# When a recurrent mixer asks for its next activation tiles: four of seven moved to hops of the recurrence, and one weight quarter moved into the next step

## The chip, the cores and the metric

The kernel runs on one core of one Trainium2 chip. The metric is the device time of one execution in microseconds. Three executions of the kernel before took 4308.31, 4318.29 and 4321.34 us, so the time before is their median, 4318.29 us. The profile is of a fourth execution, which took 4331.43 us.

## What the kernel computes

One layer of a streaming encoder over 2048 tokens of 1024 channels: a token mixer and then a mixture of experts. The change lies in the mixer, whose core is this (cut from the reference):

```python
h = rms_norm(x, norm1_gain[l]) * (1.0 + sc1) + sh1
p = h @ w_in                                   # 1024 -> 8 slices of 1024 columns, and 256 low-rank ones
...                                            # token shift, gates, decays from these slices
def step(state, inp):
    r_t, w_t, k_t, v_t, kk_t, a_t = inp
    sa = jnp.einsum('bhvk,bhk->bhv', state, kk_t)
    state = (state * w_t[:, :, None, :]
             - sa[..., None] * (kk_t * a_t)[:, :, None, :]
             + v_t[..., None] * k_t[:, :, None, :])
    y = jnp.einsum('bhvk,bhk->bhv', state, r_t)
    return state, y
...
merged = jax.nn.sigmoid(ga) * y_conv + jax.nn.sigmoid(gb) * y_rwkv
return merged @ w_out, v_first
```

## The kernel before

Five engines run streams of their own, written out by hand: TensorE (PE in the profile), VectorE (DVE), ScalarE (ACT), GpSimd (POOL), and SyncE (SP), which issues nearly all DMAs in order. They meet only at semaphores.

The mixer runs in 32 steps, `i = ct * 4 + g`: `ct` is one of 8 tiles of 128 channels (two heads), `g` one of 4 groups of 512 tokens. I call a step with `g = 3`, after which the channel tile changes, a *turn step* (3, 7, 11, ... 27), and count steps from 0. A step has two parts on TensorE.

- **Projections.** Eight slices of `h @ w_in`, in four pairs `pr`. A pair is one 2x2 block product done with seven half-size products (`proj(i, pr, n)`, n = 0 to 6, line L1082), which read seven activation tiles `hs[:, n]` (512 KB each, fetched from the DRAM tensor `h_s`) and seven weight tiles of `w[:, pr]`. Four weight tiles are loaded (`load_pair`, four DMAs of 256 KB), three more are sums that GpSimd makes from them (`mix_weights`, counted by `w_step`). All four pairs read the same `hs` tiles, so `hs[:, n]` is free for the next step after `proj(i, 3, n)`. The low-rank products L1010 and L1014 (`zdec`, `zaaa`) open a step, and L1044 and L1034 (`bonus`, `gup`) close the projections.
- **Recurrence.** `inverse_and_recurrence` interleaves two things: the triangular inverses of this step's 8 chunks of 64 tokens (L1203 to L1222), and the chunk-by-chunk recurrence of the step before, whose 24 *hops* are `x`, `u`, `sy` for chunks 0 to 7. Hop `u` of a chunk ends with L1131 and raises `u_done`. All of it is small 64x64 products, some 1500 matrix instructions and weight loads in a recurrence against about 510 in the projections.

SP's stream for a step is `load_step`: after `zaaa` it asks for `WAc` (low-rank input of the next step); in a turn step for the next channel tile's weights, pair by pair as the projections free them; then it stores `merged_s`; then it asks for the seven `hs` tiles as pair 3 frees them; in a turn step for pair 3's weights; and after `gup` for `GDc`. The stream of VectorE is a hardware loop over two steps, so it jumps back (L2310) at the start of an even step.

Of the kernel before, what the change touches and what calls it, by code (L numbers as in the profile page):

```python
# [21 lines left out]
NC = G // C  # L22
# [79 lines left out]
def build(nc, io, out):  # L102
    ctx = ExitStack()
    with ctx:
# [12 lines left out]
        S = {n: ctx.enter_context(nc.semaphore(n)) for n in names}  # L117
# [342 lines left out]
        def first(i):  # L460
            return isinstance(i, int) and i == 0
# [18 lines left out]
        def prior2(i):  # L480

            return None if isinstance(i, int) and i < 2 else i - 2
# [32 lines left out]
        def prod_count(i, pr, n):  # L515

            return i * 4 * NPROD + pr * NPROD + n + 1
# [9 lines left out]
        def _(sp):  # L527
# [24 lines left out]
            def load_pair(pr, ct):  # L552
                for slot, row, col in ((W_A11, 0, 0), (W_A12, 1, 0), (W_S3, 0, 1), (W_A22, 1, 1)):
                    sp.dma_start(w[:, pr, slot], w_cols[:, row * KH:row * KH + KH, ds(ct * P + PAIR_COLS[pr][col], P)])\
                        .then_inc(w_in_sem[pr], 16)
# [12 lines left out]
            def load_h(g, n):  # L568
                sp.dma_start(hs[:, n].rearrange("p k t -> p (k t)"), h_s[g, n]).then_inc(h_in_sem[n], 16)

            def load_ups(ct):
                sp.dma_start(UP[0:64, 0, :], io["decay_up"][0, :, ds(ct * P, P)]).then_inc(S["ups_in"], 16)
                sp.dma_start(UP[64:128, 1, :], io["aaa_up"][0, :, ds(ct * P, P)]).then_inc(S["ups_in"], 16)

            def load_gate(ct):
                sp.dma_start(UP[:, 2, :], io["gate_up"][0, :, ds(ct * P, P)]).then_inc(S["gate_in"], 16)
# [45 lines left out]
            def load_step(ct, g, final=False):  # L622
                i = ct * NG + g
                nxt = (g + 1) % NG
                turn = g == NG - 1 and not final
                if not final:
                    sp.wait_ge(S["zaaa_done"], i + 1)
                    if turn:
                        load_ups(ct + 1)
                    sp.dma_start(WAc[:, :], rank_s[0, :, nxt * G:nxt * G + G]).then_inc(S["wa_in"], 16)  # L630
                if turn:
                    for pr in range(3):
                        sp.wait_ge(S["proj_done"], prod_count(i, pr, NPROD - 1))
                        load_pair(pr, ct + 1)
                if prior2(i) is not None:
                    sp.wait_ge(S["merged_ready"], i - 1)
                    pct, pg = (ct, g - 2) if g >= 2 else (ct - 1, g + 2)
                    sp.dma_start(merged_s[ds(pct * P, P), pg * G:pg * G + G], mg[:, :]).then_inc(S["merged_out"], 16)
                if not final:
                    for n in range(NPROD):  # L640
                        sp.wait_ge(S["proj_done"], prod_count(i, 3, n))
                        load_h(nxt, n)
                if turn:
                    load_pair(3, ct + 1)
                if not final:
                    sp.wait_ge(S["gup_done"], i + 1)
                    if turn:
                        load_gate(ct + 1)
                    sp.dma_start(GDc[:, :], rank_s[1, :, nxt * G:nxt * G + G]).then_inc(S["gd_in"], 16)

            for g in range(NG):
                load_step(0, g)
            with sp.Fori(1, KT - 1) as ct:
                for g in range(NG):
                    load_step(ct, g)
            for g in range(NG):
                load_step(KT - 1, g, final=g == NG - 1)
# [1975 lines left out]
```

## Time and profile before

| | before |
|---|---|
| median of 3 executions | 4318.29 us |
| profiled execution: its time, its span | 4331.43 us, 4329.7 us |
| TensorE matmul busy | 4013.8 us (93% of the span) |
| matmuls, weight loads on TensorE | 36219, 36219 |
| VectorE, ScalarE, GpSimd busy | 1834.9, 1337.7, 471.7 us |
| the chain that ended last, by engine | PE 88%, issue 5%, DVE 3%, DMA 2% |
| seven-product projections (L1082), matmul busy | 1169.1 + 483.8 us |
| first and last start of L1082 | 141.1 and 2772.8 us |

The mixer takes the time from about 140 to about 2810 us. The rest is preparation ahead of it, and output projection, routing and experts behind it, none of which the change touches. In this profile "issue" is time in which an engine waited for nothing that the profile shows.

### The profile page before, as it was taken

Reading aid. Unit: us, or ns where it says so; the run is one execution under the profiler, and the core shown is the slowest. Engines: PE = TensorE matmul, PEld = TensorE weight load, DVE = VectorE, ACT = ScalarE, POOL = GpSimd, SP = SyncE. Lnnn points to the kernel's source line nnn. Section 1 sums busy time; section 2 is a strip of 40 time slices with the busy share of each in tenths; the row PEclk is TensorE's granted clock in tenths of the full one; section 3 lists DMA queues with packets and bytes.
Section 4 is the critical chain, followed back from the end, with each engine's and each line's share of the span. In section 5 each row is a group of like instructions: output and inputs, shape, how many; then the busy total and the mean of one; then the engine's idle time right before and its main releaser. Section 6 shows DMA issues by size and latency. Waiting matters only on the chain.

```text
span 4329.7 us, 93193 instructions
## 1 busy us (share of the span) xinstructions
PE 4013.8 (93%) x36219; PEld 2787.4 (64%) x36219; DVE 1834.9 (42%) x3767; ACT 1337.7 (31%) x3011; POOL 471.7 (11%) x522
## 2 busy tenths in 40 slices
PE   7899999999999999999999999999689999999992
PEld 4678777777777777787787887744344444444440
DVE  5445555554554554555555555422611111111115
ACT  5224334333333433333343333344211111111114
POOL 1101201210210210201201201000000000000003
PEclk9999999999999999999999999999789999999996
DMA  9612312211221221221211212234389999999999
GB/s 374 221 43 64 101 46 63 99 46 56 77 77 47 82 82 47 82 79 47 85 62 63 86 45 80 78 103 136 130 348 411 411 412 411 411 411 412 411 411 378
DMA packets 292930, 760.52 MB, mean 176 GB/s; under 512 B 16466, under 2 KB 107828, under 8 KB 292532
## 3 DMA queue, kind: packets, MB, share of 16 engines
q1 hardware_dynamic: 273876, 687.60, 42.7%
q0 software_dynamic: 11520, 41.95, 2.5%
q10 hardware_dynamic: 7136, 25.23, 1.4%
q8 instruction: 303, 4.96, 0.5%
q14 instruction: 95, 0.78, 0.1%
HBM read 679.19 MB, written 75.52 MB: 174 GB/s over the span
## 4 chain that ended last, share of the span: by engine, by line
PE 88%; issue 5%; DVE 3%; DMA 2%; ACT 1%; SPq 1%; POOL 0%; DVEq 0%; POOLq 0%; ACTq 0%
PE duo L1082 25%; PE bank L1457 10%; PE bank L1082 10%; PE bank L1461 5%; PE bank L1487 5%; PE bank L1313 5%; PE bank L1491 3%; PE duo L1211 2%; PE duo L1209 2%; PE duo L1188 2%; PE duo L1182 1%; PE bank L1145 1%; PE bank L1129 1%; PE duo L1438 1%; PE bank L1131 1%
## 5 line engine op out<-in xcount | busy, mean ns | idle before, releaser
L1082 PE MATMUL duo<-hs,w 128*128 128x256 f32 x5120 | 1169.1, 380 | 4.8 <-issue 2.4
L1082 PEld LDWEIGHTS duo<-hs,w 128*128 128x128 f32 x5120 | 968.9, 190 | 192.3 <-issue 37.3
L1082 PE MATMUL bank<-hs,w 128*128 128x256 f32 x2048 | 483.8, 379 | 0.0
L1457 PE MATMUL bank<-W,xT 128*128 128x512 f32 x1024 | 447.1, 595 | 2.2 <-DVE xT L2541 1.5
L1082 PEld LDWEIGHTS bank<-hs,w 128*128 128x128 f32 x2048 | 389.1, 190 | 52.9
L1457 PEld LDWEIGHTS bank<-W,xT 128*128 128x128 f32 x1024 | 192.9, 191 | 233.7 <-issue 233.7
L1523 ACT ACT_TABLE_LOAD x254 | 325.9, 1283 | 11.2 <-issue 6.3
L2547 DVE TENSOR_TENSOR gsig<-bank,gsig 128x512 f32<-128x512 f32 x48 | 33.2, 692 | 674.1 <-ACT gsig L1523 674.1
L1461 PE MATMUL bank<-W,xT 128*64 128x512 f32 x1024 | 227.2, 598 | 18.5 <-issue 18.5
L839 POOL TENSOR_TENSOR Tm<-Tm,idents 128x512 f32<-128x512 f32 x32 | 40.6, 1270 | 1849.2 <-DVE Tm L2255 1849.2
L1313 PE MATMUL bank<-wo,mT 128*128 128x512 f32 x512 | 233.7, 603 | 0.1
L1523 ACT ACTIVATE gsig<-bank 128x512 f32<-128x512 f32 x48 | 28.7, 598 | 659.2 <-PE bank L1457 424.2
L1487 PE MATMUL bank<-W,aT 128*128 128x512 f32 x512 | 225.1, 593 | 0.0
L1523 ACT ACTIVATE su<-duo 128x256 f32<-128x256 f32 x128 | 49.2, 384 | 436.9 <-PE duo L1082 436.9
L1461 PEld LDWEIGHTS bank<-W,xT 128*64 128x64 f32 x1024 | 76.1, 137 | 158.1 <-issue 158.1
L2271 DVE TENSOR_TENSOR Zm<-duo,mlevs 128x512 f32<-128x512 f32 x160 | 110.4, 690 | 137.1 <-PE duo L1209 137.0
L1487 PEld LDWEIGHTS bank<-W,aT 128*128 128x128 f32 x512 | 94.8, 190 | 107.9 <-issue 107.9
L2261 DVE TENSOR_TENSOR Tm<-Tm,duo 128x256 f32<-128x256 f32 x256 | 98.7, 417 | 149.9 <-PE duo L1211 149.9
L1313 PEld LDWEIGHTS bank<-wo,mT 128*128 128x128 f32 x512 | 93.8, 191 | 104.1 <-issue 102.6
L2558 DVE TENSOR_TENSOR ysb<-bank,g2b 128x512 f32<-128x512 f32 x96 | 61.8, 686 | 224.6 <-PE bank L1487 147.0
L1523 ACT ACTIVATE xsb<-bank 64x64 f32<-64x64 f32 x248 | 54.2, 218 | 296.2 <-PE bank L1104 296.2
L1209 PE MATMUL duo<-Tm,LTb 64*64 64x64 f32 x5120 | 130.2, 233 | 13.8 <-issue 11.8
(429 smaller groups left out, 6304.4 us busy)
## 6 DMA issues: line engine op xcount, KB each, us to landing
W<-in_w_expert_in_dram SPq DMA_DIRECT2D x128, 2048.0 KB, 25.4
W<-in_w_expert_out_dram SPq DMA_DIRECT2D x64, 2048.0 KB, 25.5
hs<-h_s SPq DMA_DIRECT2D x224, 512.0 KB, 4.5
w<-in_w_in_dram SPq DMA_DIRECT2D x128, 256.0 KB, 4.2
adaw<-in_w_ada_dram SPq DMA_DIRECT2D x12, 2048.0 KB, 13.4
y_s<-ysb ACTq DMA_DIRECT2D x48, 512.0 KB, 6.7
xt<-in_x_dram SPq DMA_DIRECT2D x16, 512.0 KB, 11.0
WAc<-rank_s SPq DMA_DIRECT2D x32, 256.0 KB, 3.2
```

The source lines that it names most:

```text
L1082: ins = mm(place(pr, n), w[:, pr, n, k, :], hs[:, n, k, :], start=n < 4 and k == 0, stop=k == KH - 1, skip_group_check=True)
L1188: ins = tr(bk[:, k % 2 * P:k % 2 * P + P], Tm[:, 2 * k:2 * k + 2, :].rearrange("p h t -> p (h t)"), ident[:, :])
L1209: ins = mm(one, LTb[p][rows, e, HD:2 * HD], Tm[rows, 2 * k + h, :], start=True, stop=True)
L1211: ins = mm(one, Qm[p][rows, slot_of(c), :], Zm[rows, slot_of(c), :], start=True, stop=True)
L1313: ins = mm(banks[2 * s + j][:, :], mT[:, s, k, :], wo[:, k, j * 512:j * 512 + 512], start=k == 0, stop=k == KT - 1)
L1457: ins = mm(GU[half][:, :], xT[:, slot, kk_, :], ring_rows(parts[0])[:, k, cols], start=kk_ == 0, stop=kk_ == KT - 1)
L1461: ins = mm(GU[half][lane, :], xT[:, slot, kk_, lane], ring_rows(r)[:, k, cols], start=kk_ == 0, stop=kk_ == KT - 1)
L1487: ins = mm(Y2[j][:, :], aT[:, slot, k * P:k * P + P], ring_rows(parts[0])[:, k, cols], start=k == 0, stop=k == DE // P - 1)
L1491: ins = mm(Y2[j][lane, :], aT[:, slot, k * P:k * P + P][:, lane], ring_rows(r)[:, k, cols], start=k == 0, stop=k == DE // P - 1)
L1523: return nc.scalar.activation(o, i, f, **kw)
L2261: ins = V.tensor_tensor(T_of(b), T_of(b), bk, ALU.subtract)
L2271: V.tensor_tensor(Zm[:, :, :].rearrange("p (b c) t -> p b c t", b=2), DUO[pair_of(u)][:, :, 0:4 * HD].rearrange("p b (c t) -> p b c t", t=HD),
```

## The change

It alters only SP's stream. In every step but the first, `hs` tiles 0, 1 and 2 of the next step are asked for as before, when pair 3 has read the old ones; tiles 3, 4, 5 and 6 are asked for when hop `u` of chunks 0, 2, 4 and 6 is done, inside the recurrence. `GDc`, queued behind them, moves with them. Pair 3's weights of the next channel tile are no longer asked for at the end of the turn step, but in the following step, right behind `WAc`.

```diff
                     sp.dma_start(WAc[:, :], rank_s[0, :, nxt * G:nxt * G + G]).then_inc(S["wa_in"], 16)
+                if g == 0 and not first(ct):
+                    load_pair(3, ct)
                 if turn:
                     for pr in range(3):
                         sp.wait_ge(S["proj_done"], prod_count(i, pr, NPROD - 1))
...
                     for n in range(NPROD):
-                        sp.wait_ge(S["proj_done"], prod_count(i, 3, n))
+                        if n < 3 or first(i):
+                            sp.wait_ge(S["proj_done"], prod_count(i, 3, n))
+                        else:
+                            sp.wait_ge(S["u_done"], i * NC - NC + 2 * (n - 3) + 1)
                         load_h(nxt, n)
-                if turn:
-                    load_pair(3, ct + 1)
                 if not final:
                     sp.wait_ge(S["gup_done"], i + 1)
```

The order of the other engines' instructions stays as it is. Two places of SP's queue show what moved. First a plain step (step 2, ahead of the loop over channel tiles), before; `hs` are the activation tiles, `merged_s` the stored result, `WAc` and `GDc` the low-rank inputs:

```order
L630 DMA WAc<-rank_s 128x512 [waits zaaa_done]
L638 DMA merged_s<-mg 128x512 [waits merged_ready]
L569 DMA hs<-h_s 128x1024 [waits proj_done] x7
L649 DMA GDc<-rank_s 128x512 [waits gup_done]
```

and of the change:

```order
L630 DMA WAc<-rank_s 128x512 [waits zaaa_done]
L640 DMA merged_s<-mg 128x512 [waits merged_ready]
L569 DMA hs<-h_s 128x1024 [waits proj_done] x3
L569 DMA hs<-h_s 128x1024 [waits u_done] x4
L652 DMA GDc<-rank_s 128x512 [waits gup_done]
```

Four of the seven requests now wait for the recurrence, and `GDc` stands behind the last of them. Second, the end of the first turn step (step 3) and what follows it, one piece of the difference; `w` are the weight tiles of pair 3 and `merged_s` the stored result:

```order
-L638 DMA merged_s<-mg 128x512 [waits merged_ready]
-L569 DMA hs<-h_s 128x1024 [waits proj_done] x7
-L554 DMA w<-in_w_in_dram 128x4x128 x4
+L640 DMA merged_s<-mg 128x512 [waits merged_ready]
+L569 DMA hs<-h_s 128x1024 [waits proj_done] x3
+L569 DMA hs<-h_s 128x1024 [waits u_done] x4
```

In the rows of the change for step 4, the same four requests stand behind `WAc`:

```order
L630 DMA WAc<-rank_s 128x512 [waits zaaa_done]
L554 ISA
L554 DMA w<-in_w_in_dram 128x4x128
L554 ISA
L554 DMA w<-in_w_in_dram 128x4x128
L554 ISA
L554 DMA w<-in_w_in_dram 128x4x128
L554 ISA
L554 DMA w<-in_w_in_dram 128x4x128
```

The 1 MB of weights leaves the turn step's recurrence and stands at the start of the next step's projections, without a wait of its own.

## Rows read from the trace of the kernel before

**Rows 1.** The page: chain by engine, and the queue of TensorE's instruction loads

```profile
PE 88%; issue 5%; DVE 3%; DMA 2%; ACT 1%; SPq 1%; POOL 0%; DVEq 0%; POOLq 0%; ACTq 0%
...
q8 instruction: 303, 4.96, 0.5%
```

**Rows 2.** TensorE's waits, whole run: line, cause, us, times, longest

```profile
PE bank L1148 <- issue: 26.8, 11, 4.0
...
PE duo L1209 <- issue: 11.8, 14, 1.5
...
PE duo L1182 <- DVE GKb L2257: 6.2, 11, 1.9
...
PE duo L1082 <- issue: 2.4, 8, 0.4
```

**Rows 3.** Recurrence's edges, L1034 to next L1010: steps 13, then 15

```profile
L1034 PE MATMUL bank<-GDc,UP x2: 592/592/592, 1282.2 to 1282.6; 128*128 128x512 f32 x2
...
L1010 PE MATMUL duo<-WAc,UP x2: 589/641/693, 1309.8 to 1310.3; 64*128 64x512 f32 x2
...
L1034 PE MATMUL bank<-GDc,UP x2: 592/592/592, 1446.0 to 1446.5; 128*128 128x512 f32 x2
...
L1010 PE MATMUL duo<-WAc,UP x2: 589/641/693, 1479.1 to 1479.7; 64*128 64x512 f32 x2
```

**Rows 4.** Timeline of SP's queue around those recurrences: start, us, what

```profile
1271.13 10.68 SPq L569 DMA_DIRECT2D hs<-h_s  x7
1283.21 0.32 SPq L649 DMA_DIRECT2D GDc<-rank_s  x1
...
1445.89 2.95 SPq L554 DMA_DIRECT2D w<-in_w_in_dram  x4
```

**Rows 5.** DMA traffic in 40 slices: 1283.1 to 1310 us, then 1447 to 1480

```profile
GB/s 238 402 216 268 76 0 0 0 12 0 0 0 24 0 0 0 0 0 0 24 0 0 0 0 0 24 0 0 0 0 0 0 24 0 0 0 0 0 0 24
...
GB/s 283 292 320 295 310 312 292 255 93 6 15 5 0 20 0 0 0 0 0 0 0 20 0 0 0 0 0 20 0 0 0 0 0 20 0 0 0 0 20 0
```

**Rows 6.** TensorE's timeline at the stall of step 15

```profile
1452.19 0.28 PE L1148 MATMUL bank<-ut,tok 64*64 64x64 f32 x2
1456.45 0.26 PE L1148 MATMUL bank<-ut,tok 64*64 64x64 f32 x1 [3.99 <-issue]
```

**Rows 7.** Windows: us, busy by engine, granted clock (PEclk), DMA, GB/s

```profile
1283.10:1309.80 26.70, 24.86 (x719) 20.47 (x718) 15.26 (x36) 9.60 (x42) 6.19 (x6) 1.00 0.10 34
...
1456.00:1462.00 6.00, 5.55 (x112) 4.65 (x112) 1.28 (x4) 1.42 (x6) 4.44 (x4) 0.50 0.01 4
```

**Rows 8.** TensorE's timeline, step 13: hop u of chunks 0, 2, 4, 6

```profile
1284.62 0.22 PE L1131 MATMUL bank<-xs,Qm 64*64 64x64 f32 x1
...
1291.60 0.30 PE L1131 MATMUL bank<-xs,Qm 64*64 64x64 f32 x3
...
1298.28 0.33 PE L1131 MATMUL bank<-xs,Qm 64*64 64x64 f32 x3
...
1304.43 0.30 PE L1131 MATMUL bank<-xs,Qm 64*64 64x64 f32 x3
```

**Rows 9.** L569, the activation loads of the whole run

```profile
DMA to landing us min/median/max: 3.2/4.5/15.0
```

**Rows 10.** VectorE's jump back, its first sums in step 8; weight loads

```profile
L2310 DVEq COMPARE_BRANCH  x15: 55/63/63, 477.3 to 2809.8; - x15
...
815.35 0.42 DVE L2106 TENSOR_TENSOR su<-su,duo 128x256 f32<-128x256 f32 x1 [3.51 <-ACT su L1523]
...
818.02 0.42 DVE L2111 TENSOR_TENSOR su<-su,bank 128x256 f32<-128x256 f32 x1 [0.48 <-PE bank L1082]
...
w<-in_w_in_dram SPq DMA_DIRECT2D x128, 256.0 KB, 4.2
```

**Rows 11.** Last step's recurrence, 2774 to 2808 us: traffic, TensorE's longest wait

```profile
GB/s 0 0 48 183 371 414 410 434 400 405 414 400 429 410 405 301 238 283 189 240 360 339 331 330 405 289 395 405 434 210 22 0 19 0 0 0 0 0 0 19
...
PE bank L1120 <- issue: 3.1, 2, 2.5
```

## The prediction, made before the changed kernel ran

> **What bounds the kernel now.** I read the chain that ended last first, then TensorE's waits, then two recurrences side by side. The chain is TensorE for 88% [rows 1]: a change of the mixer is worth what it takes off TensorE's idle or slowed time there. In the projections there is nothing to take: all 7168 products of L1082 stood idle for 2.4 us [rows 2]. What is left sits in the recurrence: L1148 waited 26.8 us in 11 waits, up to 4.0 us, and L1209 11.8 us in 14, both with the cause "issue" [rows 2], so for no semaphore. An engine that waits for no semaphore and no operand waits for its own instructions. The queue that loads TensorE's instructions moved 303 blocks of 4.96 MB in all, 16 KB each [rows 1], which at 72,438 matmuls and weight loads is one block for some 240 of them. The recurrence uses such a block up in about 4 to 5 us.
>
> Compare steps 13 and 15. Step 13 is plain: L1034 at 1282.2, the next step at 1309.8, 27.6 us. Step 15 is a turn step: 1446.0 to 1479.1, 33.1 us, 5.5 us more for the same instructions [rows 3]. In step 13 the seven `hs` requests and `GDc` are out by 1283.5 [rows 4] and their traffic ends about 3.4 us into the window (5 slices of 0.67 us). After it stand lone slices of 24 GB/s, which over 0.67 us is 16 KB: the instruction blocks, at slices 12, 19, 25, 32 and 39, so 4.0 to 4.7 us apart [rows 5]. In step 15 the four weight DMAs follow [rows 4], traffic of about 300 GB/s goes on for 7 us, until about 1454 [rows 5], and TensorE stops from 1452.5 to 1456.45 [rows 6]. It starts again 2.5 us after the traffic has drained. I read this as a block that was asked for at the start of the recurrence and served late behind data. The stop costs more than itself: behind it the granted clock is 0.50, 1.2 GHz, against 1.00 in step 13 [rows 7]. 5.5 us longer for a stop of 4.0 is 1.37 to 1.
>
> The Trainium skill ("Runtime: NRT & Kernel Launch", Instruction fetch mechanics) has it that instructions come in 16 KiB blocks of 256 and that only two such lines are held; the trace's 16 KB slices agree.
>
> **The change part by part.**
>
> *Gain: the first block of a recurrence.* With tiles 3 to 6, `GDc` and the weights gone from the seam, the last traffic ahead of the recurrence is tile 2, asked for some 8 us ahead of it (seven requests took 10.7 us [rows 4]; landing is 3.2 us when idle, 4.5 at the median [rows 9]). So it is down well before, and the first block meets no data. The 11 stops of L1148 then go. By the pair of steps they are worth 26.8 x 1.37 = 36.7 us. Part of it comes back: without the stop, TensorE reaches L1182 early and waits there for VectorE, 6.2 us in 11 waits [rows 2], about 0.5 each, so 11 x 0.5 = 5.5. Gain 31 us. Lower bound 26.8 - 5.5 = 21, no clock effect; upper bound 36.7 + 11.8 = 48, if the shorter stops of L1209, in even steps, go as well. I count L1209 at nothing: its stops are 0.8 us each, little more than the 0.5 us wait for VectorE at L1182 that stands right behind it and would take up what they free.
>
> *Cost A: tiles in the middle of the recurrence.* In step 13 hop `u` of chunks 0, 2, 4 and 6 ends at 1284.8, 1291.9, 1298.6 and 1304.7 [rows 8]. A tile is down 3.2 us after it is asked for [rows 9], and by the first slices of an idle queue its packets fill about the last 2 us of that: 1286 to 1288, 1293 to 1295, 1299.8 to 1301.8, 1305.9 to 1307.9. The blocks stand at slices 12 (1291.2), 19 (1295.9), 25 (1299.9), 32 (1304.6) and 39 (1309.3) [rows 5]. The first two tiles fall between blocks. The third, `hs` tile 5, starts when the fourth block does. One block per step meets one tile, and the block of slice 19 may be asked for during tile 4. The recurrence has almost no slack there, as blocks come every 4.0 to 4.7 us and are used as fast, so a delay is a stop. Lower bound: nothing. Upper bound: the block waits for most of a tile, 1.5 us in each of 30 steps, 45 us. The nearest row is the last step: there loads of about 400 GB/s ran through nearly the whole recurrence, and TensorE's longest wait for "issue" was 3.1 us in two pieces [rows 11]; with a block in 5 us or so, that is some six blocks and 0.5 us each, under much denser traffic than one 512 KB tile. I take about half of it, 0.3 us, for one block per step: 30 x 0.3 = 9 us.
>
> *Cost B: pair 3's weights at the start of seven steps (4, 8, ... 28).* Who waits for them: GpSimd's sums, then `proj(i, 3, 0)`. Four loads of 256 KB, 4.2 us each at the median [rows 10], and four sums are over within some 15 us, pair 3 starts some 40 us into the step (three quarters of the 52 us that L1082 takes per step, (1169.1 + 483.8) / 32): hidden. What they meet is another thing. All seven are even steps, and there VectorE has just jumped back to its loop's start [rows 10] and needs a fresh block before its next instruction. Its first sum of step 8 starts at 815.35 after 3.5 us idle, and 0.48 us of idle is all it then has left before the next sum, which waits for TensorE [rows 10]. TensorE's fourth and fifth products wait for these sums, so every delay of that block beyond about 1 us stops TensorE in the projections. Lower bound nothing: the block is asked for before the first weight packet moves. Upper bound as in step 15, 4.0 us in 7 steps, 28 us. I take 0.7 x 7 = 5 us: the block leads the weights, so it should overtake most of them.
>
> The Trainium skill (same page and section) states that a taken branch whose target is not held forces a load before execution goes on. By that rule Cost B is real in each of the seven steps; the trace agrees in that VectorE stands at its loop's start, but without traffic of this size beside it.
>
> *At nothing.* `GDc` is asked for some 22 us later and needed at the next `gup`, 50 us on. Tile 6 is asked for at 1304.7 and down at 1308; its first reader is the seventh product of the next step, 11 us past 1309.8. If the recurrence did not cover it, it would cost 3.2 us a step. SP itself waits longer in its queue, and behind the last tile stand only `GDc` and the next step's `WAc`, due past the recurrence.
>
> *Sum.* -31 + 9 + 5 = -17 us. Against the profiled execution's own 4331.4 that is 4314.4; the three timed ones have their median 13.1 us lower, 4318.3, and with the same -17 it comes to 4301.
>
> **The rivals.**
>
> *Collisions eat the gain.* Tile 5 delays its block by 1.0 us in each of 30 steps: 30 - 31 + 5 = +4, 4322. For it: the two coincide to 0.1 us, in every step alike, as both follow TensorE's progress. Against it: the last step's small waits [rows 11].
>
> *Collisions win (slower).* The same mechanism at 1.5 us, the rest of the tile, and each stop drags the clock as in step 15: 30 x 1.5 x 1.37 = 62, less 31, plus 5 is +36, 4354. It decides from about 1.1 us of delay per step with the clock effect ((31 + 13 - 5) / 30 / 1.37 = 0.95 for +0.3%). Against it: a tile's 512 KB in 2 us is 260 GB/s, where the last step's traffic runs at 400 and more [rows 11].
>
> *The weights strand VectorE.* Cost B at 28 us and Cost A at 9: +6, 4324; with A at nothing, 4315.
>
> *It does nothing.* If a block never waits behind data, the stops have another cause and stay. Then the change gives 0, 4318. Against it: the longest stop of L1148 anywhere, 4.0 us [rows 2], is that of step 15 [rows 6], a turn step, and only those have weights in that place.
>
> The Trainium skill ("DMA: Bandwidth & Descriptors", Queues, rings and completion order) says that a DMA engine alternates between its queues packet by packet, at most 64 descriptors at a time. By that rule a block never waits for more than a packet and this rival would hold; the 4.0 us stop under the densest traffic speaks against so short a wait.
>
> **How the numbers follow.** Three timed runs of this kernel spread over 13 us, so 0.3%, 13 us, is what can be told: faster is below 4305, slower above 4331. Chances: forecast 0.45, with a range of its own of 4283 to 4311 (gain 48 to 21, costs 14), of which 0.38 is below 4305; L1209's stops gone too and no costs, 4275 to 4283, 0.08; gain eaten 0.17, mostly within 0.3%; collisions win 0.13; weights strand VectorE 0.09, half of it slower; nothing 0.08. Faster 0.46, same 0.32, slower 0.22. The predicted time is 4301. The range leaves out the best 5% and the worst half of the collisions: 4278 to 4336.
>
> **What would show it.** Gain right: L1148's "issue" wait falls from 26.8 to under 5 us, and turn recurrences come to within 1 us of plain ones, 27 to 28 us. Cost A right: "issue" waits of under 0.5 us at the block end behind chunk 5, more than before; wrong: over 1 us each and granted clock 0.50 behind them. Cost B right: L1082's idle grows from 2.4 to some 7 us, in steps 4 to 28; wrong: 20 us or more there, ended by VectorE's sums. What would make it wrong at large: blocks delayed not by queued data but by how they are asked for, so that a single tile at the wrong moment costs as much as seven.

## The result

The changed kernel is slower. Six executions took 4344.53 to 4379.82 us, median 4373.23; six of the kernel before, on the same chip, 4308.31 to 4321.34, median 4314.31. The medians are 59 us apart. The ratio on record, which is not simply that of the two medians, is 1.012, with a 95% interval of 1.0094 to 1.0145: some 52 us more (41 to 63). I had forecast 4301, with 4278 to 4336 as the range; the measured time lies outside it and on the other side of the kernel before.

### The profile after

The profiled execution has a span of 4369.8 us, 40.1 more than before. In the changed kernel the lines below the edit stand three further down, so that L1148 of before is L1151, L1155 is L1158, L1104 is L1107, L1209 is L1212 and L1082 is L1085. TensorE's waits over the whole run, with us, times and longest, which answer to [rows 2]:

```profile
PE duo L1212 <- issue: 26.5, 15, 2.1
PE bank L1151 <- issue: 21.0, 11, 3.4
PE bank L1158 <- issue: 17.7, 14, 1.6
...
PE bank L1107 <- issue: 12.0, 14, 1.3
...
PE duo L1085 <- DVE su L2109: 2.8, 1, 2.8
...
PE duo L1085 <- issue: 0.4, 2, 0.2
```

Four places are to be told apart. L1151 and L1212 are the two products at which the first block of a recurrence runs out, in odd and in even steps. Together they waited 38.6 us before and 47.5 now: L1151 has lost 6 us, L1212 has gained 15. L1107 and L1158 stand at the start of chunk 6, where the fourth block runs out. They waited 0 and 6.1 us before, and 29.7 now. The projections are hardly touched: L1085's two rows make 3.2 us, and 2.8 of that is one wait. Before it was 4.5 us, as two waits for VectorE (1.5 and 0.6 us) stand beside the 2.4 us of [rows 2].

Stops are not all of it. The windows view of both mixers, from their first low-rank product to the end of their last hop `u`, with the columns of [rows 7]. The kernel before:

```profile
140.00:2850.10 2710.10, 2585.98 (x30549) 2126.44 (x30549) 1387.16 (x2907) 999.13 (x2358) 353.31 (x312) 0.98 0.22 70
```

and the changed kernel:

```profile
139.20:2887.50 2748.30, 2607.71 (x30549) 2147.33 (x30549) 1393.38 (x2907) 999.69 (x2358) 353.01 (x312) 0.97 0.22 69
```

The mixer is 38 us longer, which is nearly the whole difference. Of these, 22 us are TensorE's own busy time for the same 30549 matmuls (2607.71 - 2585.98), at a granted clock of 0.97 against 0.98. The other 16.5 are idle time.

Now one recurrence, step 13 again, which took 27.6 us before [rows 3]. Its edges, by the lines view (`gup`, and the first product of the next step):

```profile
L1037 PE MATMUL bank<-GDc,UP x2: 592/592/592, 1293.5 to 1293.9; 128*128 128x512 f32 x2
...
L1013 PE MATMUL duo<-WAc,UP x2: 589/641/693, 1324.4 to 1325.0; 64*128 64x512 f32 x2
```

SP's timeline (start, duration), with the loads in its queue:

```profile
1282.44 36.21 SPq L569 DMA_DIRECT2D hs<-h_s  x7
1318.71 0.42 SPq L652 DMA_DIRECT2D GDc<-rank_s  x1
```

The traffic from 1294.4 to 1324.4 us in 40 slices of 0.75 us:

```profile
GB/s 0 0 0 60 235 377 49 11 0 0 0 22 0 0 153 344 202 0 22 0 0 0 0 229 350 142 0 0 0 0 0 0 0 208 344 336 172 11 0 22
```

TensorE's timeline at its two stops:

```profile
1301.53 0.21 PE L1151 MATMUL bank<-ut,tok 64*64 64x64 f32 x1 [1.60 <-issue]
...
1316.19 0.32 PE L1107 MATMUL bank<-tok,GKb 64*64 64x64 f32 x2 [1.03 <-issue]
```

And the windows behind the second stop, to where the recurrence is nearly over:

```profile
1316.20:1317.50 1.30, 1.30 (x42) 1.13 (x42) 0.26 (x1) 0.30 (x2) 0.00 (x0) 1.00 0.00 0
1317.00:1319.50 2.50, 2.46 (x69) 2.13 (x60) 0.76 (x3) 0.82 (x4) 0.00 (x0) 0.69 0.08 25
1319.50:1322.00 2.50, 2.50 (x32) 1.89 (x28) 1.29 (x3) 0.78 (x3) 0.00 (x0) 0.63 0.81 291
```

It takes 30.9 us now. The traffic shows the four tiles as four bumps, as the change intends. Two of the lone 22 GB/s slices, 16 KB over 0.75 us, stand free (slices 11 and 18, the second and third block), and one at the end. The first and the fourth block are not to be seen alone in these slices: they lie under the bumps of tile 3 (slices 3 to 6, 1296.7 to 1299.7) and tile 5 (slices 23 to 25, 1311.7 to 1313.9). The DMA view of two narrow windows takes tile 5's bump apart, queue by queue (packets, MB, share of the engines). From 1311.6 to 1313.85 us it has one row of a queue:

```profile
q1 hardware_dynamic: 144, 0.52, 72.0%
```

and in the next microsecond, 1313.85 to 1314.85, again one:

```profile
q8 instruction: 1, 0.02, 5.9%
```

So the 16 KB block is a single packet of the instruction queue, q8, and it starts when all 512 KB of the tile have been started. With tile 3 it is the same (1296.9 to 1299.26 us the tile alone, the block at 1299.27). TensorE stops once for each of these two blocks, and starts again 2.3 us after the last packet of the tile. Behind the second stop the granted clock falls to 0.69 and 0.63, so part of each of these windows ran at 1.2 GHz, where [rows 7] has 1.00 for the whole of this recurrence before.

### The profile page after: what moved, and what is told of

It is laid out like the page before. It is cut to its first block, busy times and chain, and to the rows that moved or that the text cites. A ratio compares the mean times of both kernels' runs of the same rounds, so it can differ in the third digit from the quotient of the medians.

```text
span 4369.8 us, 93193 instructions
## 1 busy us (share of the span) xinstructions
PE 4042.3 (93%) x36219; PEld 2810.0 (64%) x36219; DVE 1842.3 (42%) x3767; ACT 1338.3 (31%) x3011; POOL 472.8 (11%) x522
## 4 chain that ended last, share of the span: by engine, by line
PE 89%; issue 4%; DVE 3%; DMA 2%; ACT 1%; SPq 1%; POOL 0%; DVEq 0%; ACTq 0%; POOLq 0%
PE duo L1085 25%; PE bank L1460 10%; PE bank L1085 10%; PE bank L1464 5%; PE bank L1490 5%; PE bank L1316 5%; PE bank L1494 3%; PE duo L1214 2%; PE duo L1212 2%; PE duo L1191 2%; PE duo L1185 2%; PE bank L1148 1%; PE bank L1132 1%; PE duo L1441 1%; PE bank L1134 1%
## 5 line engine op out<-in xcount | busy, mean ns | idle before, releaser
L1085 PE MATMUL duo<-hs,w 128*128 128x256 f32 x5120 | 1169.9, 380 | 3.5 <-DVE su L2109 2.8
L1085 PEld LDWEIGHTS duo<-hs,w 128*128 128x128 f32 x5120 | 970.1, 190 | 189.4 <-issue 33.8
L1085 PE MATMUL bank<-hs,w 128*128 128x256 f32 x2048 | 483.8, 379 | 0.0
L1085 PEld LDWEIGHTS bank<-hs,w 128*128 128x128 f32 x2048 | 389.1, 190 | 52.9
L1526 ACT ACTIVATE gsig<-bank 128x512 f32<-128x512 f32 x48 | 28.7, 598 | 662.4 <-PE bank L1460 424.9
L1212 PE MATMUL duo<-Tm,LTb 64*64 64x64 f32 x5120 | 138.0, 240 | 28.1 <-issue 26.5
```

The source lines that it names most:

```text
L1085: ins = mm(place(pr, n), w[:, pr, n, k, :], hs[:, n, k, :], start=n < 4 and k == 0, stop=k == KH - 1, skip_group_check=True)
L1212: ins = mm(one, LTb[p][rows, e, HD:2 * HD], Tm[rows, 2 * k + h, :], start=True, stop=True)
L1526: return nc.scalar.activation(o, i, f, **kw)
```

## The experiments

All keep the full computation. Each was timed beside runs of the kernel before on the same chip, but not all on one chip: the kernel before took 4320.45 us beside the two halves and the two kernels of the section behind them, 4315.62 beside the kernels with one tile moved and those with all four tiles in other places, and 4319.65 beside the one with tiles 5 and 6 together and the last two. A ratio is against these. Where I set kernels of different chips against each other, I give the difference of the medians and, where it matters, that of the ratios.

### Each half of the change by itself

First the weights alone, the tiles as before (against the kernel before):

```diff
+                if g == 0 and not first(ct):
+                    load_pair(3, ct)
...
-                if turn:
-                    load_pair(3, ct + 1)
```

> Only the weight part: pair 3's weights in the following step, all seven tiles asked for at the end of the projections as before. Theory (a tile that is asked for at hop u of chunks 0 and 4 delays the instruction block that is due there; the weights' move is good): the recurrences of the seven turn steps fall from 30.6 us on average to about 27.5, the others stay, so 15 to 25 us faster than before (ratio 0.994 to 0.9965). Rival (the weights at the start of a step are what costs, as they strand VectorE after its jump back): slower than before, projections of steps 4, 8, ... longer by 2 us or more.

It took 4294.41 us (4293.43 to 4295.51), ratio 0.9939 [0.992, 0.9959]: 26 us faster. Its waits, with the line numbers of before:

```profile
PE duo L1209 <- issue: 11.4, 14, 1.9
...
PE bank L1148 <- issue: 10.4, 11, 2.3
...
PE bank L1155 <- issue: 4.7, 12, 0.7
```

L1148 fell from 26.8 to 10.4 us, L1209 stayed. That the weights' move is good holds, and the rival is out. In the seven turn steps L1148 waited 20.8 us before and 5.0 now, and their recurrences took 28.7 us on average, where they had taken 31.5.

Then the tiles alone, the weights at the end of the turn step:

```diff
-                if g == 0 and not first(ct):
-                    load_pair(3, ct)
...
+                if turn:
+                    load_pair(3, ct + 1)
```

(against the changed kernel).

> Only the tile part: tiles 3 to 6 at hops u of chunks 0, 2, 4, 6, pair 3's weights at the end of the turn step as before (now behind tile 6). Theory (hops): as slow as the whole change, ratio 1.010 to 1.014, since the first instruction block of a recurrence is late in some 20 steps and the fourth in nearly all. Rival (weights cost): close to before, within 0.3%.

4362.88 us (4355.56 to 4372.25), ratio 1.0092 [1.007, 1.0114]. The loss is that of the tiles; the rival, that it is that of the weights, is out. The ratio is a little below the 1.010 that I had set as the lower end. The interval meets that of the whole change (1.0094 to 1.0145), so with the tiles inside the recurrence the weights' move no longer gives anything that can be told: as I read it, a first block that is late behind tile 3 in any case leaves nothing to free.

### Is it the hop, or that data move in the recurrence at all?

Against the changed kernel, tile 3 goes back to the end of the projections:

```diff
-                        if n < 3 or first(i):
+                        if n < 4 or first(i):
                             sp.wait_ge(S["proj_done"], prod_count(i, 3, n))
                         else:
-                            sp.wait_ge(S["u_done"], i * NC - NC + 2 * (n - 3) + 1)
+                            sp.wait_ge(S["u_done"], i * NC - NC + (2, 4, 6)[n - 4] + 1)
```

> The changed kernel with tile 3 asked for at the end of the projections again, so that only tiles 4, 5, 6 wait for hops u of chunks 2, 4, 6. Theory (each tile costs by where it meets a block): the first block comes at 2.3 us into the recurrence in nearly all steps, the waits at its end (the issue waits of the 64x64 product L1209 and of the state product) fall by some 35 us, the stop behind chunk 5 stays; time within 0.3% of before (ratio 0.998 to 1.003). Rival (any 512 KB inside the recurrence costs the same, wherever it is put): three quarters of the loss stays, ratio 1.009.

4337.0 us (4328.24 to 4340.29), ratio 1.0035 [1.0021, 1.005]: 36 us less than the changed kernel, between the two expectations, and nearer to the theory's. The first block's two places waited 21.8 us in all, 26 less than the changed kernel's 47.5, where I had expected some 35 less.

The next kernel differs from it by two numbers, `(2, 5, 7)` in place of `(2, 4, 6)`.

> As the kernel with tile 3 early, and tiles 5 and 6 moved one hop u on, to chunks 5 and 7, so that tile 5's packets no longer start together with the fourth block. Theory (meeting a block): the stops at the start of chunk 6 (0.8 to 1.3 us in nearly every step) go, 15 to 30 us faster than before (ratio 0.993 to 0.9965). Rival (any data inside the recurrence costs): as slow as the kernel with tile 3 early, ratio 1.009.

4294.42 us (4285.68 to 4299.54), ratio 0.9943 [0.9921, 0.9965]. The same three tiles, at other hops, are worth 43 us. Its waits (line numbers as after) have L1107 no longer with "issue" as cause, and the first block's two places at 12.0 us together:

```profile
PE duo L1212 <- issue: 8.7, 10, 1.3
...
PE bank L1158 <- issue: 4.3, 14, 0.5
PE bank L1151 <- issue: 3.3, 2, 1.8
```

The rival, that data inside the recurrence cost as such, is out.

### One tile at a time

In these two, the weights are moved, six tiles and `GDc` are asked for as before, and one tile is asked for last, at one hop. They differ from the weights-only kernel in nothing else:

```diff
                     for n in range(NPROD):
-                        sp.wait_ge(S["proj_done"], prod_count(i, 3, n))
-                        load_h(nxt, n)
+                        if n != 3 or first(i):
+                            sp.wait_ge(S["proj_done"], prod_count(i, 3, n))
+                            load_h(nxt, n)
...
                     sp.dma_start(GDc[:, :], rank_s[1, :, nxt * G:nxt * G + G]).then_inc(S["gd_in"], 16)
+                    if not first(i):
+                        sp.wait_ge(S["u_done"], i * NC - NC + 0 + 1)
+                        load_h(nxt, 3)
```

> The weights-only kernel (4294 us) with one tile moved: tile 3 is asked for at hop u of chunk 0, all else, GDc too, at the end of the projections. Theory (a tile at that hop meets the first instruction block): slower than weights-only by the first block's stops, 10 to 30 us, so 4305 to 4325. Rival (only the number of bytes inside the recurrence counts): a quarter of the change's loss, 4307 at most; or nothing, since the seam was full of data anyhow.

4324.3 us (4313.17 to 4338.72), ratio 1.0026 [1.0011, 1.0041], against 4294.4 for weights-only: 30 us for one tile in one place (38 by the ratios). Its waits (lines four further down than before):

```profile
PE duo L1213 <- issue: 21.0, 14, 2.1
PE bank L1152 <- issue: 18.9, 10, 3.1
```

With tile 5 at hop `u` of chunk 4 in the same manner:

> The weights-only kernel with tile 5 alone at hop u of chunk 4. Theory (its packets start with the fourth block): stops of 0.8 to 1.3 us at the start of chunk 6 in nearly every step, 30 to 45 us slower than weights-only, 4325 to 4340. Rival (it is the sum of several tiles in one recurrence that lets the blocks fall behind): within 10 us of weights-only.

4339.85 us (4323.52 to 4355.74), ratio 1.0063 [1.0045, 1.0081]: 45 us for one tile (54 by the ratios).

```profile
PE bank L1159 <- issue: 18.3, 14, 1.6
...
PE bank L1108 <- issue: 12.5, 14, 1.3
```

That is the chunk 6 stop by itself, in its full size: 30.8 us (18.3 + 12.5) against 29.7 in the changed kernel. It needs neither tile 3 nor tile 4.

### Does a block wait for a packet or for all that is queued?

The same with tile 6 right behind tile 5 at the same hop: `for n in (5, 6): load_h(nxt, n)`.

> As the kernel with tile 5 alone at hop u of chunk 4 (4340 us, 28 stops of 1.1 us), but with tile 6 right behind tile 5 at the same hop, so 1 MB meets the fourth block in place of 512 KB. Theory (a block waits behind all data queued ahead of it): the stops at chunk 6 grow to some 2.3 us each, 4370 to 4385. Rival (a block waits for the packets in front of it alone, and then goes ahead of the rest): the stops stay at 1.1 us, 4330 to 4350.

4384.63 us (4377.81 to 4398.54), ratio 1.0151 [1.0134, 1.0168]. The same two products, five lines further down than before:

```profile
PE bank L1160 <- issue: 35.6, 14, 2.9
PE bank L1109 <- issue: 25.4, 14, 2.1
```

61.0 us in 28 stops in place of 30.8, so 2.2 us each against 1.1: twice the data, twice the stop. The DMA packets of the two traces show why. In step 13 of this kernel the two tiles move from 1316.17 us, and the window from 1316.1 to 1319.86 has

```profile
q1 hardware_dynamic: 287, 1.05, 85.5%
q8 instruction: 1, 0.02, 1.6%
```

287 of the tiles' 288 packets, and then the block at its very end. Over the recurrences of steps 2 to 29, the fourth block started when 509 of 512 KB had been started on average with tile 5 alone, 2.0 us behind the tile's first packet, and when 949 of 1024 KB had been with both tiles, 3.05 us behind it. So the block went behind nearly all that was queued, and not behind one packet.

### All four tiles in other places

`(2, 5, 7, 7)` for tiles 3 to 6 in the changed kernel:

```diff
-                            sp.wait_ge(S["u_done"], i * NC - NC + 2 * (n - 3) + 1)
+                            sp.wait_ge(S["u_done"], i * NC - NC + (2, 5, 7, 7)[n - 3] + 1)
```

> All four tiles stay inside the recurrence, as in the change, but at hops u of chunks 2, 5, 7, 7 in place of 0, 2, 4, 6. Theory (where a tile meets a block decides, not that it is there): as fast as the kernel with tiles 4 to 6 at 2, 5, 7, 4285 to 4298. Rival (four tiles in the recurrence cost by their number): 4340 or more.

4301.56 us (4296.21 to 4315.82), ratio 0.9977 [0.9961, 0.9992]: 72 us less than the changed kernel (62 by the ratios) with as many tiles asked for inside the recurrence, and 3.6 us above the expected range. Then `(7, 7, 7, 7)`:

> All four tiles asked for together at hop u of chunk 7, the last. Theory: the recurrences are free of stops behind chunk 5 and at the first block, 27 to 28 us long, but the four tiles and GDc are still moving when VectorE has jumped back at the start of an even step, so its block is late there: projections of even steps 1 to 3 us longer, 4295 to 4320. If VectorE's block is not delayed by data, the projections stay at 54.1 us and the time is 4280 to 4290.

4309.29 us (4301.57 to 4313.95), ratio 0.9989 [0.9976, 1.0002]. The chunk 6 stop is gone. The first block's stops are not, though the expectation had them gone:

```profile
PE duo L1212 <- issue: 16.8, 15, 1.9
...
PE bank L1151 <- issue: 12.5, 8, 2.3
```

That is 29.3 us, against 38.6 before and 21.8 in the weights-only kernel, although only tiles 0 to 2 move ahead of a recurrence here and the last of them is down 1.5 to 3.8 us before it starts. In the projections VectorE shows what the theory said. VectorE's first sum in the even step 8, and TensorE's waits for VectorE in the projections:

```profile
815.38 0.42 DVE L2109 TENSOR_TENSOR su<-su,duo 128x256 f32<-128x256 f32 x1 [5.90 <-issue]
```

```profile
PE duo L1085 <- DVE T L2116: 5.5, 12, 0.6
...
PE duo L1085 <- DVE su L2109: 2.3, 3, 1.6
```

5.90 us idle, with "issue" as the cause, against 3.51 in [rows 10], where the profile names ScalarE as what ended the wait. Counted from the start of the step, an 8 KB instruction packet moved at 6.0 us against 3.7, and the sum followed it by some 2 us in both: the block after the jump back is 2.4 us later. TensorE then waits in twelve of the even steps, 0.5 us each, so the loss was smaller than the 1 to 3 us that I expected: their projections took 54.1 us on average, against 53.4 before.

### What is left of the first block's lateness

Weights-only, with `GDc` and the gate weights asked for at the start of the step that needs them, so that 256 KB less move when a recurrence begins:

```diff
+                if not first(i):
+                    sp.wait_ge(S["zaaa_done"], i + 1)
+                    sp.wait_ge(S["gup_done"], i)
+                    if g == 0:
+                        load_gate(ct)
+                    sp.dma_start(GDc[:, :], rank_s[1, :, g * G:g * G + G]).then_inc(S["gd_in"], 16)
...
-                if not final:
-                    sp.wait_ge(S["gup_done"], i + 1)
-                    if turn:
-                        load_gate(ct + 1)
-                    sp.dma_start(GDc[:, :], rank_s[1, :, nxt * G:nxt * G + G]).then_inc(S["gd_in"], 16)
```

> The weights-only kernel with the last 256 KB of the seam taken away too: GDc and the gate weights are asked for at the start of the step that needs them. Theory (the first block is late through what data still moves at the start of the recurrence): the first stops fall from 17 us to some 9, as in the kernel with tiles at 2, 5, 7; 4280 to 4292. Rival (what is left of the first block's lateness has no data behind it): as weights-only, 4290 to 4300.

4295.81 us (4291.62 to 4303.84), ratio 0.995 [0.9937, 0.9964], the same as weights-only. The rival's range holds it, and the first block's two places waited 27.5 us (21.8 in weights-only), where the theory wanted some 9. The last is tile 6 with `GDc` at hop `u` of chunk 2 (`n < 6`, `(2,)[n - 6]`):

> The changed kernel with tile 6 alone (and GDc behind it) moved, to hop u of chunk 2, which lies just behind the second block; tiles 3 to 5 at the end of the projections. Theory (phase): fewer data at the seam than in weights-only and one tile in a free place: 4282 to 4294. Rival: the tile and GDc, 768 KB there, reach into the third block's time: 4300 to 4315.

4297.7 us (4292.08 to 4312.43), ratio 0.9958 [0.9943, 0.9973], which lies between the two ranges and cannot be told from weights-only. No kernel was found that is clearly below 4294 us.

## Why the prediction was wrong

**What bounds the kernel: right.** TensorE's stops without a semaphore are late instruction blocks. Every kernel that moved data against a block moved the stop at that block's end, the stop doubled with the data, and the packets show the block starting behind the tile. One support was not what it was taken for: the section of the Trainium skill that the prediction names for two held lines ("Runtime: NRT & Kernel Launch", Instruction fetch mechanics) has them for a memory of 32 KiB, and gives TensorE 128 KiB. The runs show no reserve of that size: with tile 5 alone the fourth block started 20.6 us into the recurrence on average, against 19.3 in weights-only, and this 1.3 us became a stop of 1.1.

**Gain, 31 us: right in part.** The weights alone gave 26 us. But L1148's wait fell by 16.4 us and not by the 26.8 that the sum took, so the size is partly luck. A stop was priced at 1.37 from one pair of steps, and the pair was an extreme one: the longest of the seven turn recurrences against the shortest of all. Before the change the turn recurrences took 31.5 us on average and the other odd ones 29.4. And 6.0 of L1148's 26.8 us lay in plain steps, which have no weights in that place.

**"The first block meets no data": wrong.** This sentence cleared the traffic ahead of the recurrence and did not look at what the change puts right behind its start. In step 13, counted from the start of the recurrence, the first block moved at 3.5 us before; tile 3's packets now move from 3.6 to 5.8 us, and the block behind them. Alone the tile costs 30 us. It took back what the tiles' removal from the seam could give.

**Cost A, "one block per step: 30 x 0.3 = 9 us": the step that failed.** "The first two tiles fall between blocks" placed tile 3 wrongly, since the first block is hidden under the traffic in [rows 5] and I read only the visible ones. For tile 5 the place was right, to a few tenths of a us, and the price wrong: 1.1 us per stop in 28 steps, 45 us of time, where I took 0.3 and 9. With both, 75 us (30 + 45; 91 by the ratios); the whole change stands 79 above weights-only (78 by the ratios). Tiles 4 and 6 cost nothing that can be told: tiles 4, 5, 6 together (4337.0) are no slower than tile 5 alone (4339.9).

The price came from [rows 11], the last step, where much denser traffic gave 3.1 us of waits. That row was the nearest in kind of traffic but not in the state of TensorE. Part of that stretch ran at 1.2 GHz, since its granted clock was 0.80 (the same window of the kernel before):

```profile
2774.00:2808.00 34.00, 29.52 (x714) 23.86 (x714) 15.65 (x36) 9.90 (x43) 6.08 (x6) 0.80 0.70 238
```

And I had divided its waits by some six blocks, a number that no row showed. The trace has the blocks at 2780.9, 2787.8, 2795.1, 2801.8 and 2807.8 us, some 7 us apart, and only the first three fall into the dense traffic: 3.1 us over three blocks is 1.0 us each, close to what tile 5 cost. Step 15's stop was a second good row: 4.0 us, behind the 1.3 MB asked for last or the 2.0 MB that [rows 5] shows in its window. At the same rate 512 KB is 1.0 to 1.5 us, and the upper end was my upper bound.

**Cost B, 5 us: nothing in the changed kernel.** L1085 waited 2.8 us once for VectorE, and 0.4 for "issue" where it was 2.4 before. Over seven steps that is not the 5 us of the sum. The delay itself was there: in steps 4, 8, ... 28 the weights, asked for behind `WAc`, made VectorE's first sum start 0.4 to 0.8 us later, counted from the step's start. In step 20:

```profile
1835.21 0.42 DVE L2109 TENSOR_TENSOR su<-su,duo 128x256 f32<-128x256 f32 x1 [4.38 <-issue]
```

It was 3.58 us of idle time in the same step before. No product of TensorE waited for it, which agrees with the prediction's "about 1 us" that it can bear. With four tiles and `GDc` moving at the jump back the same block was 2.4 us later, and TensorE waited.

**The rivals.** "Collisions win" was the case that came true, at +52 us where it said +36, and I had given it 0.13. It named 1.5 us a stop in 30 steps times 1.37, less the gain; it was 1.1 us at the fourth block in 28 steps, and 1.8 at the first in 26 (1.5 in 25 before). Its threshold was put too high: the sum that stands beside "about 1.1 us" gives 0.95. "It does nothing" is out by the doubled stop and by weights-only.

**What stays open.** The first block is late in part of the steps even where nothing moves. With tiles at 2, 5, 7 the last early tile is down 0.2 to 2.3 us before the recurrence, and TensorE still stops 12.0 us at the first block's end. With all four at hop 7 the first block started anywhere from 3.2 to 6.0 us into the recurrence, with no data ahead of it. Taking `GDc` away changed nothing. What decides this was not tried, and what bounds the first block is settled only as far as tile 3 and the weights go.

## What to carry to other kernels

When a tight stretch of short instructions waits for "issue", count its instructions against the instruction queue's blocks, find in the traffic slices when each block is due, and put DMAs in the gaps. Asking for two tiles one chunk later was worth 43 us here, more than the whole reordering could bring. Bound such a collision from above by the size of the transfer divided by the rate that it moves at (here 2.2 us for 512 KB, where the stop was 1.1), not by the waits of a stretch that runs at another clock. Try the parts of a change one by one: here one half by itself was worth 26 us, and adding the other to it cost 79. And look at the busy time of a stretch too, not at its stops alone.

## What was unexpected of the hardware

A block of 16 KB of instructions does not slip in ahead of data that another queue has already handed over. 512 KB in front of it cost TensorE 1.1 us, 1 MB 2.2 us, and in the trace the block's packet starts when the data ahead of it have been started, nearly to the last packet. The Trainium skill ("DMA: Bandwidth & Descriptors", Queues, rings and completion order) has a DMA engine change between its queues after each packet of at most 64 descriptors. By that a block would wait no longer for 1 MB than for 512 KB, if a tile's share of an engine is one packet; these two runs do not agree with that: with two tiles queued, 949 of 1024 KB went first.

A stop costs more than its own length, and by no fixed factor. The whole mixer of weights-only, in the windows view:

```profile
139.60:2812.20 2672.60, 2567.03 (x30549) 2111.51 (x30549) 1389.79 (x2907) 998.67 (x2358) 353.54 (x312) 0.99 0.22 71
```

and with tile 3 moved to hop `u` of chunk 0:

```profile
138.50:2844.50 2706.00, 2594.26 (x30549) 2135.89 (x30549) 1389.30 (x2907) 999.67 (x2358) 352.65 (x312) 0.97 0.23 70
```

Of the 33 us between them only 6 are idle time. The other 27 are busy time for the same matmuls, at a granted clock of 0.97 against 0.99. With tile 5 instead it was 27 us of idle and 15 of busy time, and from the kernel before to weights-only 19 and 19. These are single profiled executions. Why a stop at the first block costs so much more clock than one at the fourth was not tried.
